# Attention stage of a two-block layer: scores issued three pairs ahead instead of two, four buffers for the unscaled probabilities

## The chip, the cores and the metric

The kernel runs on one core of a Trainium2 chip. The metric is the device time of one execution in microseconds (us), as the median of several runs. Engines are named as the profile names them: PE is the matrix engine (PEld its weight loads), DVE the vector engine, ACT the scalar engine, POOL the GpSimd engine, SP the engine that issues most transfers.

## The reference

The program computes two transformer blocks on 512 tokens of width 1024, in float32. The first block is a feed-forward network, a hybrid mixer, and a second feed-forward network. The second block is a pooling and mLSTM layer. The change lies in the mixer alone, in its softmax attention, which is this part of the reference:

```python
s = jnp.einsum('bqgrd,bkgd->bgrqk', qs, kw).astype(f32)
s = s - slopes[:, :, None, None] * dist_w.astype(f32)
s = jnp.where(mask_w, s, NEG_INF)
p_w = jax.nn.softmax(s, axis=-1)
o_win = jnp.einsum('bgrqk,bkgd->bqgrd', p_w.astype(vw.dtype), vw)
...
o = gb[..., 0:1] * o_cmp + gb[..., 1:2] * o_slc + gb[..., 2:3] * o_win
```

There are 8 query heads in 2 groups of 4, head size 64. With 512 tokens both the selected branch and the window branch are plain causal attention, each over its own keys and values, and each is multiplied by its own gate. A third, compressed branch adds one small product per head. Beside them stands a gated linear attention of 4 heads, worked in chunks of 64 tokens.

## The kernel before, in words

The program is written by hand for each engine: every engine has its own list of instructions, which it works in order, and semaphores join the lists. Nothing is scheduled by a planner, so the order in the loops below is the order on the chip.

Most of the time goes to the dense products. Their weights arrive by SP in units of 512 KB, ACT makes the rounded high half (w_hi, line 1162), POOL the rest (w_lo, line 471), and PE runs three products for each (lines 516 to 518).

The attention stage works on 32 pairs. PAIRS (line 346) runs over the head j of a group (4), the branch b (2) and the block qt of 128 queries (4). A pair is the same work for both groups g. Its width w is (qt + 1) * 128 keys, so the widths 128, 256, 384, 512 recur in turn: pair m has width 128 when m is a multiple of 4, and 512 when m leaves 3. The steps of pair m are:

- scores(m) on PE (line 772): queries by keys into the bank ps[:, g]. There is one bank for each group, so the scores of pair m wait until the maxima of pair m - 1 have been taken (neg_done, line 771).
- negative(m) on DVE (line 1847): reads that bank, adds the distance bias, writes the negated score to a buffer prob and its minimum to nmax. The buffers are a ring of RING pairs, so negative(m) also waits for the turn of pair m - RING (line 1846). At the first pair of each head, biases(j) (line 1835) rewrites the bias first.
- exponent(m) on ACT (line 1348): the exponential in place, its sum to psum_l.
- finish(m) on DVE (lines 1857 and 1861): reciprocal of the sum, then scale by it and by the gate.
- turn(m) on PE (line 786): transposes of 128x128 into the bank ps[:, 2 + g]. It waits for finish(m), and for the copy of pair m - 1 out of the same bank.
- copy(m) on ACT (line 1359): from that bank to one of three buffers for turned probabilities.
- values(m) on PE (line 796), two pairs after the turn. The eighth pair of each head adds the compressed product (line 804). Before the next head's first values, PE waits for the head's result to leave the bank: head_of on ACT (line 1364), then tail_of on DVE (line 1867).

The steps of the linear attention are dealt out among the first 24 pairs by linear(m), six slots for each block of 128 tokens. In it ACT takes squares (line 1370), DVE masks and copies (lines 1874, 1891, 1897), and after pair 23 ACT takes a square root (line 1375), for which it loads another function table and then the exponential's table again. Then POOL scales the result (line 490), and PE turns it (line 856).

The loop of each engine over m (before the change; lines 879, 1382 and 1927) is:

- PE: scores(m + 2), linear(m), values(m - 2), turn(m). In the pairs with m % 8 == 2 (m > 2) the turn comes before the values. At m = 0, after the scores, PE also turns the linear values 2 and 3.
- ACT: exponent(m + 2), at m = 0 the two copies of the turned linear values (line 1309), copy(m), and what falls to this m of head_of, the squares, the root.
- DVE: finish(m), at m = 0 the last projection tile, tail_of where due, negative(m + 2) with biases where a head begins, linear(m).

Scores 0 and 1, and their maxima and exponentials, are taken earlier, beside the last projection tiles.

Of the kernel before, what the change touches and what calls it, by code (L numbers as in the profile page):

```python
# [38 lines left out]
NH, NG, DH = 8, 2, 64  # L39
# [21 lines left out]
    return t if t < MT_Q else t - HPG  # L61


RING = 3
POOL_ADDS = 4
PV_BANK = 4
HALF_BANK, ADD_BANK = 5, 7
# [69 lines left out]
def build(nc, dram, out):  # L137
    with ExitStack() as ctx:
# [14 lines left out]
        scr = sb("scr", [P, DC, T])  # L153
# [42 lines left out]
        w1 = sb("w1", [P, 2, CMP_BLOCK // 2, CMP_HID], F32, own)  # L196
        own.close()
        pc_t = sb("pc_t", [P, NH, T], F32, mixer)
        third_t = pc_t[:, 4:4 + NG, :]
        gel_four, pc_t = pc_t[:, NG, 0:NG * HPG * NC32].rearrange("p (g n) -> p g n", g=NG), pc_t[:, 0:NG, :]  # L200
        own = ExitStack()
        gtmp = sb("gtmp", [P, 8, T], F32, own)
# [11 lines left out]
        c_sum = sb("c_sum", [P, TT * NH], F32, mixer)  # L214
        nmax = sb("nmax", [P, 2 * RING], F32, mixer)
        psum_l = sb("psum_l", [P, 2 * RING], F32, mixer)
# [61 lines left out]
        kst_tok = proj[:, 0:2, :].rearrange("p a t -> p (a t)").rearrange("p (q d) -> p q d", q=TT)  # L278
        k_in, q_in = proj[:, kept(MT_GK):kept(MT_GK) + 2, :], proj[:, kept(MT_GQ):kept(MT_GQ) + 2, :]
        o_tok = proj[:, kept(MT_GV):kept(MT_GV) + GH, :]  # L280
        square_junk = scr[:, 2 * RING, :]
        gated_v = proj[:, kept(MT_GR):kept(MT_GR) + GH, :]

        rows_of = [d_mat[:, 0, :], d_mat[:, 1, :], h_sum[:, 0, :], h_sum[:, 1, :]] + [
# [62 lines left out]
        NPAIR = len(PAIRS)  # L347
        PER_J = NPAIR // HPG
# [155 lines left out]
        def _(pe):  # L504
# [271 lines left out]
            def attention():  # L776
# [100 lines left out]
                        linear_turn(m - 26)  # L877

                for m in range(NPAIR):
                    if m + 2 < NPAIR:  # L880
                        scores(m + 2)
                    if m == 0:
                        pe.wait_ge(pct_done[0], 1)
                        turn_linear_values(2)
                        turn_linear_values(3)
                    linear(m)
                    late = m % PER_J == 2 and m > 2
                    if late:
                        turn(m)
                    if m >= 2:  # L890
                        values(m - 2)
                    if not late:
                        turn(m)
# [261 lines left out]
        def _(act):  # L1155
# [195 lines left out]
            def attention():  # L1351

                def copy(m):
                    w = (PAIRS[m][2] + 1) * P
                    if m >= 3:
                        act.wait_ge(pv_done, m - 2)
                    for g in range(NG):
                        act.wait_ge(turn_ready, 2 * m + g + 1)
                        nc.scalar.activation(turned(m, g)[:, 0:w], ps[:, 2 + g, 0:w], ACT.Copy
                                             ).then_inc(prob_t_done, 1)  # L1360

                def head_of(j):
                    act.wait_ge(oc_done, j + 1)
                    nc.scalar.activation(o_hi[:, j, :], ps[:, PV_BANK, :], ACT.Copy).then_inc(o_hi_done, 1)

                def linear_squares(tt):
                    act.wait_ge(a_used, 2 * tt + 1)
                    for h, m, half in HEADS_OF:
                        k, at = 2 * half + m, O_AT + m * P
                        nc.scalar.activation(square_junk[:, k * P:(k + 1) * P], ps[:, HALF_BANK + half, at:at + P], ACT.Square,  # L1370
                                             accum_out=g_col[:, tt * GH + k:tt * GH + k + 1]).then_inc(gsq_done, 1)

                def linear_root():
                    act.wait_ge(gsq_done, GH * TT)
                    nc.scalar.activation(g_col[:, :], g_col[:, :], ACT.Sqrt, scale=1.0 / GDV, bias=c_("eps")
                                         ).then_inc(grms_done, 1)

                def linear_head(h):
                    act.wait_ge(go_done, TT)
                    nc.scalar.activation(h_hi[:, 4 + h, :], gated_v[:, h, :], ACT.Copy).then_inc(go_hi, 1)  # L1380

                for m in range(NPAIR):
                    if m + 2 < NPAIR:
                        exponent(m + 2)
                    if m == 0:
                        linear_values(2)
                        linear_values(3)
                    copy(m)
                    if m % PER_J == 1 and m > 1:
                        head_of(m // PER_J - 1)  # L1390
                    if m % LIN_SLOTS == 4 and m < TT * LIN_SLOTS:
                        linear_squares(m // LIN_SLOTS)
                    if m == 23:
                        linear_root()
                    if m >= 30:
                        linear_head(m - 30)
                load_root()
                for h in range(2, GH):
                    linear_head(h)
                head_of(HPG - 1)  # L1400
# [253 lines left out]
        def _(dve):  # L1654
# [196 lines left out]
            def attention():  # L1851
# [75 lines left out]
                for m in range(NPAIR):  # L1927
                    finish(m)
                    if m == 0:
                        take(22, 23)  # L1930
                    if m % PER_J == 2 and m > 2:
                        tail_of(m // PER_J - 1)
                    if m + 2 < NPAIR:
                        if (m + 2) % PER_J == 0:
                            biases((m + 2) // PER_J)
                        negative(m + 2)
                    linear(m)
                tail_of(HPG - 1)

# [498 lines left out]
```

## Time and profile before

| | us |
|---|---|
| median of 3 runs | 1676.01 |
| lowest and highest | 1674.09, 1678.9 |
| the profiled execution | 1678.87 |
| its span, first to last instruction | 1677.1 |
| mean granted PE clock of the span | 0.995 of full |
| attention stage, on PE | about 527.8 to 622.4 |

The span is what the trace covers, and 1.77 us lie around it. All start times below count from the start of the span. In a row of the timeline the bracket at the end is the time that the engine stood idle just before the instruction, and what released it. The end of a PE instruction is modelled, and neighbouring ones overlap a little; the chain of work lists them without the overlap.

### The profile page before, as it was taken

The numbers are of one execution on the slowest core, as the hardware profiler recorded it, in microseconds if no ns is written. First come the engines' busy times: TensorE is split into PE (matmuls) and PEld (weight loads), VectorE is DVE, ScalarE is ACT, GpSimd is POOL, SyncE is SP. The second block draws the span as 40 slices with busy tenths as digits, with TensorE's granted clock in tenths as the row PEclk, the third lists the DMA queues.
The fourth block names the chain that finished last, engine by engine and source line by source line (L and its number), as shares of the span: only waits on it lengthen the run. The fifth ranks groups of instructions, "written<-read, shape, count | busy, mean of one in ns | idle before, by whom it ended". The sixth has DMA issues, their size and how long they took to land.

```text
span 1677.1 us, 22221 instructions
## 1 busy us (share of the span) xinstructions
PE 1652.7 (99%) x7820; PEld 1341.6 (80%) x7820; DVE 717.9 (43%) x1149; ACT 645.0 (38%) x998; POOL 648.7 (39%) x278
## 2 busy tenths in 40 slices
PE   7999999999999999999999999999999999999998
PEld 6888888887887668888888888888888888888886
DVE  4333330204535866333332033577678731553222
ACT  5322331323425763332232133574544522444432
POOL 3444444443332024444444444432322324444444
PEclk9999999999999999999999999999999999999999
DMA  4322332225222002232232233222112112332322
GB/s 167 100 99 89 100 100 88 100 88 176 76 80 72 2 1 88 88 100 97 91 100 100 88 100 101 88 88 76 63 63 75 63 63 88 120 106 88 100 92 96
DMA packets 41955, 149.28 MB, mean 89 GB/s; under 512 B 4784, under 2 KB 4912, under 8 KB 41648
## 3 DMA queue, kind: packets, MB, share of 16 engines
q1 hardware_dynamic: 40112, 142.37, 25.3%
q10 hardware_dynamic: 1792, 6.21, 1.1%
q8 instruction: 35, 0.57, 0.1%
q14 instruction: 16, 0.13, 0.0%
HBM read 145.41 MB, written 2.10 MB: 88 GB/s over the span
## 4 chain that ended last, share of the span: by engine, by line
PE 92%; issue 4%; DVE 2%; POOL 1%; ACT 1%; DVEq 0%; POOLq 0%; ACTq 0%
PE ps L516 21%; PE ps L517 20%; PE ps L518 20%; PE ps L622 5%; PE ps L624 5%; PE ps L623 5%; PE ps L1018 1%; PE ps L1030 1%; PE ps L772 1%; PE ps L786 1%; POOL w_lo L471 1%; PE ps L796 1%; PE ps L936 1%; PE ps L938 1%; PE ps L937 1%
## 5 line engine op out<-in xcount | busy, mean ns | idle before, releaser
L471 POOL TENSOR_TENSOR w_lo<-w_raw,w_hi 128x1024 fp32r<-128x1024 f32 x262 | 633.9, 2420 | 933.0 <-ACT w_hi L1162 925.9
L1162 ACT ACTIVATE w_hi<-w_raw 128x1024 fp32r<-128x1024 f32 x260 | 275.7, 1060 | 894.1 <-PE ps L518 650.8
L516 PE MATMUL ps<-h_hi,w_hi 128*128 128x512 f32 x1040 | 408.3, 393 | 2.3 <-POOL w_lo L471 1.8
L517 PE MATMUL ps<-h_lo,w_hi 128*128 128x512 f32 x1040 | 406.1, 390 | 0.0
L518 PE MATMUL ps<-h_hi,w_lo 128*128 128x512 f32 x1040 | 406.0, 390 | 0.0
L516 PEld LDWEIGHTS ps<-h_hi,w_hi 128*128 128x128 f32 x1040 | 195.8, 188 | 46.3 <-issue 2.8
L518 PEld LDWEIGHTS ps<-h_hi,w_lo 128*128 128x128 f32 x1040 | 195.8, 188 | 40.8
L517 PEld LDWEIGHTS ps<-h_lo,w_hi 128*128 128x128 f32 x1040 | 195.8, 188 | 40.0
L516 PE MATMUL ps<-n_hi,w_hi 128*128 128x512 f32 x512 | 207.1, 404 | 0.0
L518 PE MATMUL ps<-n_hi,w_lo 128*128 128x512 f32 x512 | 202.9, 396 | 0.0
L517 PE MATMUL ps<-n_lo,w_hi 128*128 128x512 f32 x512 | 202.8, 396 | 0.0
L624 PE MATMUL ps<-hid_hi,w_lo 128*128 (+1 forms) x352 | 139.2, 395 | 0.0
L622 PE MATMUL ps<-hid_hi,w_hi 128*128 (+1 forms) x352 | 139.1, 395 | 0.0
L623 PE MATMUL ps<-hid_lo,w_hi 128*128 (+1 forms) x352 | 139.1, 395 | 0.0
L518 PEld LDWEIGHTS ps<-n_hi,w_lo 128*128 128x128 f32 x512 | 96.8, 189 | 22.8
L1701 DVE TENSOR_TENSOR silu<-ps,r_row 128x512 f32<-128x512 f32 x44 | 30.4, 692 | 197.2 <-PE ps L518 193.8
L517 PEld LDWEIGHTS ps<-n_lo,w_hi 128*128 128x128 f32 x512 | 96.9, 189 | 22.1
L516 PEld LDWEIGHTS ps<-n_hi,w_hi 128*128 128x128 f32 x512 | 96.7, 189 | 21.9
L1716 DVE SCALAR_TENSOR_TENSOR x<-ps,x 128x512 f32<-128x512 f32 x16 | 11.1, 693 | 200.0 <-PE ps L624 199.8
L1706 DVE TENSOR_TENSOR hid_lo<-hid,hid_hi 128x512 f32 x44 | 70.8, 1610 | 40.2 <-ACT hid_hi L1220 40.2
L622 PEld LDWEIGHTS ps<-hid_hi,w_hi 128*128 128x128 f32 x352 | 66.1, 188 | 16.0
L624 PEld LDWEIGHTS ps<-hid_hi,w_lo 128*128 128x128 f32 x352 | 66.1, 188 | 16.0
(323 smaller groups left out, 1850.0 us busy)
## 6 DMA issues: line engine op xcount, KB each, us to landing
w_raw<-in_units SPq DMA_DIRECT2D x262, 512.0 KB, 3.3
x<-in_x SPq DMA_DIRECT2D x4, 512.0 KB, 7.2
w<-in_w ACTq DMA_DIRECT2D x1, 2048.0 KB, 7.8
out<-scr SPq DMA_DIRECT2D x8, 256.0 KB, 2.0
scr<-proj ACTq DMA_DIRECT2D x8, 128.0 KB, 3.9
inv_count<-in_inv_count ACTq DMA_DIRECT2D x1, 1024.0 KB, 5.1
const<-in_const SPq DMA_DIRECT2D x1, 772.0 KB, 10.2
cbias<-in_cbias ACTq DMA_DIRECT2D x1, 512.0 KB, 9.9
```

The source lines that it names most:

```text
L471: nc.gpsimd.tensor_tensor(w_lo[:, slot, :], w_raw[:, slot, :], w_hi[:, slot, :].bitcast(F32), ALU.subtract).then_inc(w_lo_done, 1)
L516: nc.tensor.matmul(ps[:, bank, :], whi, hi[:, k, :], start=(n == 0), stop=False)
L517: nc.tensor.matmul(ps[:, bank, :], whi, lo[:, k, :], start=False, stop=False)
L518: mm = nc.tensor.matmul(ps[:, bank, :], wlo, hi[:, k, :], start=False, stop=(n == DC - 1))
L622: nc.tensor.matmul(acc, w_hi[:, slot, at:at + P], mv_hi, start=start and kk == 0, stop=False)
L623: nc.tensor.matmul(acc, w_hi[:, slot, at:at + P], mv_lo, start=False, stop=False)
L624: mm = nc.tensor.matmul(acc, w_lo[:, slot, at:at + P], mv_hi, start=False, stop=stop and kk == 1)
L772: nc.tensor.matmul(ps[:, g, 0:w], queries[r, j, qt * P:(qt + 1) * P], tile_((MT_KS, MT_KW)[b])[r, 0:w], start=True, stop=True).then_inc(sc ...
L786: mm = nc.tensor.transpose(ps[:, 2 + g, at], prob[:, 2 * (m % RING) + g, at], ident)
L1162: nc.scalar.activation(w_hi[:, slot, :], w_raw[:, slot, :], ACT.Copy).then_inc(w_hi_done, 1)
L1701: chain.link(nc.vector.tensor_tensor(silu[:, f, :], ps[:, 5 + 2 * f, :], r_row[:, :], ALU.mult))
L1706: nc.vector.tensor_tensor(hid_lo[:, at, :].rearrange("p a t -> p (a t)"), hid[:, f, :], hid_hi[:, at, :].rearrange("p a t -> p (a t)").bit ...
```

## The change

RING goes from 3 to 4, and scores, maxima and exponentials run AHEAD = 3 pairs ahead of the turn. The third pair ahead is opened at m = 0, where each engine now does pair 2 and pair 3 in one go. Values stay two pairs behind the turn, with three buffers for turned probabilities as before. The ring of four pairs takes all 8 tiles of scr, so the junk output of the squares, which lay in the seventh, moves to an unused tile of pc_t. The banks are as before, and nmax and psum_l grow by 2 columns each.

```diff
-RING = 3
+RING = 4
+AHEAD = 3
...
-        third_t = pc_t[:, 4:4 + NG, :]
+        third_t, spent = pc_t[:, 4:4 + NG, :], pc_t[:, 6, :]
...
-        square_junk = scr[:, 2 * RING, :]
+        square_junk = spent
...
                 for m in range(NPAIR):
-                    if m + 2 < NPAIR:
-                        scores(m + 2)
+                    if m == 0:
+                        scores(2)
+                    if m + AHEAD < NPAIR:
+                        scores(m + AHEAD)
                     if m == 0:
                         pe.wait_ge(pct_done[0], 1)
                         turn_linear_values(2)
...
                 for m in range(NPAIR):
-                    if m + 2 < NPAIR:
-                        exponent(m + 2)
+                    if m == 0:
+                        exponent(2)
+                    if m + AHEAD < NPAIR:
+                        exponent(m + AHEAD)
                     if m == 0:
                         linear_values(2)
                         linear_values(3)
...
-                    if m + 2 < NPAIR:
-                        if (m + 2) % PER_J == 0:
-                            biases((m + 2) // PER_J)
-                        negative(m + 2)
+                    if m == 0:
+                        negative(2)
+                    if m + AHEAD < NPAIR:
+                        if (m + AHEAD) % PER_J == 0:
+                            biases((m + AHEAD) // PER_J)
+                        negative(m + AHEAD)
                     linear(m)
```

## Rows read from the trace of the kernel before

**Rows 1.** The page: busy time of each engine, share of the span, instructions
```profile
PE 1652.7 (99%) x7820; PEld 1341.6 (80%) x7820; DVE 717.9 (43%) x1149; ACT 645.0 (38%) x998; POOL 648.7 (39%) x278
```

**Rows 2.** Windows, attention stage: busy of PE, PEld, DVE, ACT, POOL; clock, DMA
```profile
527.80:622.40 94.60, 91.55 (x817) 60.21 (x816) 73.82 (x250) 70.81 (x230) 9.04 (x7) 0.98 0.02 7
```

**Rows 3.** Waits, 527 to 623: who waited for whom, us in total, times, longest
```profile
ACT scr L1348 <- DVE nmax L1847: 18.3, 24, 1.4
...
DVE scr L1847 <- PE ps L772: 8.8, 10, 2.0
```

**Rows 4.** Chain of work, 560 to 569: start, us, what; overlap taken out
```profile
560.70 0.67 PE ps L772 x4
...
562.99 0.85 PE ps L772 x4
...
565.22 0.37 PE ps L786 x2
565.59 1.08 PE ps L772 x4
...
567.12 1.02 PE ps L796 x16
568.14 0.59 PE ps L786 x4
568.73 0.42 PE ps L772 x4
```

**Rows 5.** Timeline, opening of the stage: start, us, engine, line, operation, idle before
```profile
528.82 0.56 DVE L1847 CUSTOM_DVE_ANT_0 scr<-ps,bias 128x384 f32<-128x384 f32 x1
...
529.17 2.36 POOL L471 TENSOR_TENSOR w_lo<-w_raw,w_hi 128x1024 fp32r<-128x1024 f32 x1 [4.30 <-ACT w_hi L1162]
...
529.97 2.04 DVE L1861 TENSOR_SCALAR scr<-scr,psum_l,gate_tok 128x256 f32<-128x256 f32 x2
...
530.63 1.06 ACT L1309 ACTIVATE gv_tok<-ps 128x512 f32<-128x512 f32 x2
...
531.74 0.65 PE L825 MATMUL ps<-gv_tok,proj 64*64 64x128 f32 x8 [0.65 <-ACT gv_tok L1309]
...
534.32 1.16 PE L835 MATMUL ps<-gv_tok,intra 128*128 128x128 f32 x8 [0.27 <-DVE intra L1874]
```

**Rows 6.** Groups by form, 534 to 598: count, busy us, mean ns of one, idle before
```profile
L1847 DVE CUSTOM_DVE_ANT_0 scr<-ps,bias 128x512 f32<-128x512 f32 x10 | 6.5, 689 | 4.7 <-PE ps L772 4.7
...
L1861 DVE TENSOR_SCALAR scr<-scr,psum_l,gate_tok 128x256 f32<-128x256 f32 x10 | 3.7, 410 | 0.2
...
L1348 ACT ACTIVATE scr<-scr,nmax 128x512 f32<-128x512 f32 x11 | 7.9, 724 | 3.6 <-DVE nmax L1847 3.6
```

**Rows 7.** Timeline, the other places where PE waits, before the root and after
```profile
545.84 0.88 DVE L1835 TENSOR_SCALAR bias<-const 128x512 f32<-128x512 f32 x2
...
547.10 0.91 PE L772 MATMUL ps<-proj,queries 64*128 64x256 f32 x4 [0.29 <-DVE nmax L1847]
...
560.26 0.44 PE L796 MATMUL ps<-pc_t,v_tok 128*64 128x128 f32 x4 [0.55 <-DVE o_lo L1867]
...
617.09 0.68 PEld L786 LDWEIGHTS ps<-const,scr 128*128 128x128 f32 x6 [0.35 <-DVE scr L1861]
```

**Rows 8.** Timeline around the square root, 598 to 604
```profile
598.81 1.28 ACT L1375 ACT_TABLE_LOAD   x1
...
598.94 0.30 PE L786 MATMUL ps<-const,scr 128*128 128x128 f32 x1 [0.18 <-ACT pc_t L1359]
...
600.76 2.25 DVE L1861 TENSOR_SCALAR scr<-scr,psum_l,gate_tok 128x256 f32<-128x256 f32 x2
...
602.94 0.42 ACT L1359 ACTIVATE prob_t<-ps 128x128 f32<-128x128 f32 x2
...
603.33 0.63 PE L786 MATMUL ps<-const,scr 128*128 128x128 f32 x4 [0.90 <-ACT prob_t L1359]
```

**Rows 9.** Windows, PE after that wait: length, busy, granted clock, DMA
```profile
604.00:609.00 5.00, 5.00 (x26) 0.66 0.01 2
```

## Prediction, made before the changed kernel was run

> **What bounds the kernel now.** I read the page first. PE is busy for 99% of the span [rows 1], so a change elsewhere counts only where PE waits for it. Then I cut out the attention stage, the only place that the diff touches. It lasts 94.60 us, and PE is busy in 91.55 of them [rows 2]. So PE stands idle for 94.60 - 91.55 = 3.05 us. That is the first number that matters: an edit that only lets work start earlier can win no more than this, 0.18% of the run.
>
> The busy PE might hide more, since its ends are modelled. The Trainium skill ("Perfetto Trace Analysis", Identifying the Most-Contended Engine) warns that busy matmul time is a poor measure of headroom. The chain of work answers that here: its pieces on PE follow each other without a hole, for example 565.22 + 0.37 = 565.59 [rows 4].
>
> Second, the waits of the stage. If distance were short, DVE would wait for exponentials before finish(m). No such wait is in the list. What is there is ACT waiting 18.3 us for maxima, and DVE waiting 8.8 us for scores [rows 3]. Both wait on something that comes from PE, directly or through DVE. The prefetch of two pairs is already long enough, and the helpers idle because PE paces them.
>
> Third, the timeline at each place where PE waits. There are five kinds, and their idle times are the stage's 3.05 us within rounding and overlap: the opening (0.65 and 0.27, [rows 5]), the rewritten bias (0.29), the head's result (0.55 at one head; the others show less), the last pairs (0.35 on the weight loads, some 0.2 net) [rows 7], and the square root (0.90, 0.18 and a smaller one just ahead of it, [rows 8]). After the root PE runs at a mean granted clock of 0.66 for 5 us, at 1.2 GHz for most of them [rows 9]. That costs 5 x 0.34 = 1.7 us.
>
> **The change part by part.** No instruction is added or removed: 32 pairs have the same scores, maxima, exponentials, turns and values as before, and no transfer moves. Only order changes, so every term is a difference of a wait. Scores cost 0.42, 0.67, 0.85 and 1.08 us at widths 128 to 512 [rows 4]. PE does one more pair of scores before any given turn, and gets it back at the end, so shifts by this are no cost.
>
> There is still one bank per group for scores. So scores(m + 3) must wait for negative(m + 2), which DVE issues just where it issued negative(m + 1) before: after finish(m - 1). PE's wait for maxima keeps its place. What grows is the time from exponent to finish, where nobody waits. I cost that part at nothing, in steady state. The moved junk tile and the wider nmax change no instruction's shape: nothing as well. The fourth buffer keeps negative(m + 3) waiting for turn(m - 1), the same turn as before, long done.
>
> Opening (m = 0). Now scores(3) stands ahead of the turns of linear values, negative(3) behind negative(2), and exponent(3) ahead of the two gv_tok copies. Negative(2) begins at 528.82 and takes about 1.05 for both groups, so to 529.9 [rows 5]. Scores(3) follow group by group from 529.4 to 530.5. PE meanwhile has nothing else, as its linear turns are queued behind them. Negative(3) runs 530.1 to 531.4 (2 x 0.689), exponent(3) 530.9 to 532.4 (2 x 0.724 and a read) [rows 6]. The gv_tok copies then take 1.06 [rows 5] and end near 533.5, so that L825 starts near 533.6 instead of 531.74: 1.86 later. Of this PE has used 0.42 for scores(4), which is moved work, not loss. The mask wait of 0.27 (0.35 with overlap) ends in the delay, and some 0.2 of slack between L825 and the next turn go too. Net: 1.86 - 0.42 - 0.35 - 0.2 = +0.9 us. Bounds: 0.2, if the copies come earlier than I think, to 1.6, if nothing is absorbed.
>
> On the DVE, finish(1) used to take 2.04 us here for two instructions, against 2 x 0.41 when alone [rows 5, 6]; it ran beside POOL's w_lo, which lasted to 531.5. Now finish(1) comes after negative(3), at 531.4, when POOL is done. The Trainium skill ("SBUF — State Buffer", Who interferes with whom) says that such a DVE instruction and POOL share a port pair as an exclusive lock. By that rule, the trace agrees. It saves DVE 1.2 us there, but PE waits for ACT in that stretch, so I give it nothing.
>
> Bias. The 0.88 us of biases stood between a 384-wide turn and the next scores, and PE lost 0.29 (0.36 with overlap) at one head [rows 7]. They move one pair up. There the next scores are preceded by 1.02 of 512-wide values and a turn of 0.59 [rows 4], and DVE has time: -0.3 us (0 to -0.36).
>
> Head's result. PE waits at values(8) for bank 4, 0.55 (0.63 with overlap) [rows 7]. Scores(13), 0.67, replace scores(12), 0.42, ahead of it, filling 0.25. The other two heads wait less. DVE's tail_of now delays a wider negative, which can give 0.1 back. Sum: -0.2 us (-0.5 to +0.3).
>
> Square root. ACT works without a pause from the squares of pair 22 through the root to copy(24). The queue gets exponent(26) ahead of copy(23), where 25 was, and exponent(27) ahead of copy(24), where 26 was. Each is one width step more, so +0.25 us each. The first moves with PE's own extra scores; the second delays copy(24), on which turn(25) waits at 603.33 [rows 8]. PE's own work in between shrinks, as scores(27) and scores(28), 1.08 + 0.42, replace scores(26) and scores(27), 0.85 + 1.08 [rows 4]: 0.43 less. So the wait at turn(25) grows from 0.9 to about 1.6, and net of the scores moved ahead the turn comes about +0.35 us late (0 to +0.8). DVE's finish(25), 2.25 us beside POOL [rows 8], stays the next to be late.
>
> End. No scores are left at pair 29. The wait of the last turns for finish goes away, since negative(31) no longer stands before it: -0.2 us (0 to -0.35).
>
> Sum: 0.9 - 0.3 - 0.2 + 0.35 - 0.2 = +0.55, say +0.5. Against the profiled execution's own 1678.87 that is 1679.4. That execution lies 2.86 above the median of 1676.01, and carries nothing here that the others need not have, so against the median it is 1676.5.
>
> **The rivals.**
>
> 1. All the stage's waits go, because slack on ACT and DVE grows at last: -3.05, and with no wait before it the slow clock goes too, -1.7. Together -4.75, or 1671.3. Against it: the opening and the root are waits behind queued ACT work, which the change lengthens. That the granted clock follows the wait is what [rows 8, 9] show.
>
> 2. The clock falls once more. By the times above, PE is idle in the opening for some 0.7 us before scores(3) and for 1.2 us before L825, close together, where it had 0.65 and 0.27; at 603 a wait of 0.9 came before 1.2 GHz. One more such stretch costs 1.7: 1676.5 + 1.7 = 1678.2. The Trainium skill ("TensorE: Matmul & The Clock Gate", What's actually happening) says that a monitor gates the clock by how busy PE has been. By that rule both longer waits speak against this change; it would give the same 1678.2.
>
> 3. Slower, by bunching on ACT. The 512-wide exponent now stands directly before copy(m) for m = 0, 4 ... 28, eight pairs, where before it stood at m = 1, 5 and so on. The next turn needs that copy. From the first group's scores to the end of the copy I get 0.1 + 0.69 for its maxima, 2 x 0.72 + 0.2 for the exponentials [rows 6] and 0.42 for a 128-wide copy [rows 8]: 2.85 us. In that time PE has its own work: the second group's scores 0.54, values 0.81, turn 0.37, scores 0.42, values 1.02 [rows 4] (0.81 is the 384-wide step, between 0.59 and 1.02): 3.16 us. It decides when this slack of 0.3 is gone. Should the handovers take 1.0 more, PE loses about 0.7 in each of eight pairs: +5.6, with the rest 1682.1.
>
> 4. The change doesn't do what it says: three pairs of distance exist on paper, but the single score bank keeps DVE and ACT where they were. That is contained in my forecast, and gives 1676.5 less the small terms: 1676.0.
>
> **How the numbers follow.** My forecast, with rival 4 in it: 0.69. Rival 1, or most of it: 0.12. Rival 2: 0.13. Rival 3: 0.06. The three runs before spread from 1674.09 to 1678.9, so the measured median can move by a microsecond or two without cause. The range reaches from rival 1 to somewhat under rival 3: 1671.5 to 1681.0. A measurement of this kernel can tell 0.3% from no change, that is 5.0 us. Rival 1 gives just under that, so faster has 0.04. Slower is rival 3, or rival 2 more than once: 0.06. Same: 0.90.
>
> **What would show it.** Right: in the changed trace the stage lasts 94 to 96 us. L825 first starts near 533.6, after a PE wait for gv_tok of over 1 us. The first bias no longer has PE waiting behind it. Turn(25) waits 1.3 to 2 us and the clock falls after it as before. DVE's waits for PE's scores and ACT's for maxima stay near 9 and 18 us. Wrong: an opening without a longer wait, regular waits of PE for prob_t at every fourth pair (rival 3), a second stretch at 1.2 GHz (rival 2), or a stage under 92 us (rival 1).

## The result, and the profile after

| | before | after |
|---|---|---|
| median, us | 1676.91 (20 runs) | 1679.22 (20 runs) |
| lowest and highest | 1674.09, 1678.9 | 1676.39, 1682.66 |
| the profiled execution | 1678.87 | 1681.47 |
| its span | 1677.1 | 1679.7 |

The ratio of after to before is 1.0015, with a 95% interval of 1.0009 to 1.0022. The change costs 2.3 us. That is under the 0.3% that the prediction set as its bound, but the interval leaves out 1.

The page of the changed kernel, first its span and then the busy times that answer to [rows 1]:

```profile
span 1679.7 us, 22219 instructions
...
PE 1656.1 (99%) x7820; PEld 1344.0 (80%) x7820; DVE 718.6 (43%) x1149; ACT 645.5 (38%) x998; POOL 649.8 (39%) x278
```

The counts are those of before. PE's busy time grew by 3.4 us with the same 7820 matmuls. Part of it is a lower clock, and part is waits that lie inside a row and count as busy, as the second profile of this kernel will show. The windows of the attention stage answer to [rows 2] and [rows 9]. The columns are the stretch, its length, busy time of PE, PEld, DVE, ACT and POOL, and then the granted clock:

```profile
527.20:624.90 97.70, 93.78 (x817) 62.49 (x816) 73.53 (x250) 71.06 (x230) 9.14 (x7) 0.97 0.02 7
534.00:539.00 5.00, 5.00 (x31) 3.54 (x30) 3.83 (x13) 1.99 (x8) 0.00 (x0) 0.66 0.00 2
606.00:611.00 5.00, 4.00 (x20) 2.89 (x22) 4.63 (x15) 3.90 (x14) 2.47 (x3) 0.66 0.00 2
```

The stage takes 97.7 us instead of 94.6. PE idles in 97.70 - 93.78 = 3.9 of it, where it was 3.05. And there are two stretches at a mean clock of 0.66, most of each at 1.2 GHz, where before had one: the old one behind the root and a new one at 534, behind the opening.

The waits of the stage answer to [rows 3]:

```profile
ACT scr L1351 <- DVE nmax L1852: 17.4, 22, 1.3
...
DVE scr L1852 <- PE ps L773: 10.8, 11, 2.4
```

ACT still waits for maxima and DVE for scores, for nearly as long as before. Nobody waits for an exponential, as nobody did. A third pair of distance had nothing to hide.

The timeline of the opening answers to [rows 5]. The columns are start, length, engine, line, operation, and in brackets the idle time just before and what ended it:

```profile
528.77 1.60 PE L773 MATMUL ps<-proj,queries 64*128 64x512 f32 x4 [0.65 <-DVE nmax L1852]
...
529.93 0.69 DVE L1852 CUSTOM_DVE_ANT_0 scr<-ps,bias 128x512 f32<-128x512 f32 x1 [0.74 <-PE ps L773]
...
531.36 0.73 DVE L1866 TENSOR_SCALAR scr<-scr,psum_l,gate_tok 128x256 f32<-128x256 f32 x2
...
532.09 1.06 ACT L1312 ACTIVATE gv_tok<-ps 128x512 f32<-128x512 f32 x2
...
533.20 0.65 PE L826 MATMUL ps<-gv_tok,proj 64*64 64x128 f32 x8 [1.16 <-ACT gv_tok L1312]
```

Scores(3), maxima(3) and exponent(3) all go ahead of the gv_tok copies. PE runs out of work behind scores(4) and waits 1.16 us, where it had 0.65.

The square root, which answers to [rows 8]:

```profile
604.21 2.25 DVE L1866 TENSOR_SCALAR scr<-scr,psum_l,gate_tok 128x256 f32<-128x256 f32 x2
...
605.18 0.72 ACT L1351 ACTIVATE scr<-scr,nmax 128x512 f32<-128x512 f32 x1
...
606.60 0.42 ACT L1362 ACTIVATE prob_t<-ps 128x128 f32<-128x128 f32 x2
...
607.00 1.09 PE L787 MATMUL ps<-const,scr 128*128 128x128 f32 x4 [1.70 <-ACT prob_t L1362]
```

Exponent(27), 512 wide, now stands ahead of copy(24), and turn(25) waits 1.70 us where it waited 0.90.

**Marks for the comparison.** Each head ends with a compressed product (line 804 before, 805 after), and PE works in one fixed order. So the starts of these four products, counted from the start of scores(2) at 527.87 and 527.21, cut the stage into parts that can be laid side by side. In after they stand at these lines (the timeline of PE, one line from each of four stretches):

```profile
559.42 1.07 PE L805 MATMUL ps<-pc_t,vc_tok 32*64 32x512 f32 x4
...
582.44 1.07 PE L805 MATMUL ps<-pc_t,vc_tok 32*64 32x512 f32 x4
```

The third and the fourth start at 604.23 and 623.98. Before, the starts were 556.79, 579.32, 601.36 and 621.44. This gives the following parts, in us. The columns after the first two are experiments, told below. Their parts come from their own timelines in the same way. A slow stretch behind the root lies in the last part of all but copies first, so that part, and the stage, are not like for like there.

| part, up to | before | after | after, again | copies first | four buffers alone |
|---|---|---|---|---|---|
| first product | 28.92 | 32.21 | 30.67 | 29.48 | 28.92 |
| second | 22.53 | 23.02 | 23.01 | 23.02 | 22.52 |
| third | 22.04 | 21.79 | 21.79 | 21.79 | 22.04 |
| fourth, and to the next stage | 21.08 | 20.75 | 20.84 | 19.74 | 21.06 |
| the stage | 94.57 | 97.77 | 96.31 | 94.03 | 94.54 |

The first part of the changed kernel holds one more scores step of 0.42 us than that of before, and the last part one less.

### The profile page after: what moved, and what is told of

It is laid out like the page before. It is cut to its first block, busy times and chain, and to the rows that moved or that the text cites. A ratio compares the mean times of both kernels' runs of the same rounds, so it can differ in the third digit from the quotient of the medians.

```text
span 1679.7 us, 22219 instructions
## 1 busy us (share of the span) xinstructions
PE 1656.1 (99%) x7820; PEld 1344.0 (80%) x7820; DVE 718.6 (43%) x1149; ACT 645.5 (38%) x998; POOL 649.8 (39%) x278
## 4 chain that ended last, share of the span: by engine, by line
PE 93%; issue 4%; DVE 1%; ACT 1%; POOL 1%; DVEq 0%; POOLq 0%; ACTq 0%
PE ps L517 21%; PE ps L519 20%; PE ps L518 20%; PE ps L624 5%; PE ps L625 5%; PE ps L623 5%; PE ps L773 1%; PE ps L1021 1%; PE ps L1033 1%; PE ps L787 1%; PE ps L797 1%; POOL w_lo L472 1%; PE ps L939 1%; PE ps L940 1%; PE ps L941 1%
## 5 line engine op out<-in xcount | busy, mean ns | idle before, releaser
L624 PEld LDWEIGHTS ps<-hid_lo,w_hi 128*128 128x128 f32 x352 | 66.1, 188 | 16.1
```

The lines of the kernel that those rows point to most:

```text
L624: nc.tensor.matmul(acc, w_hi[:, slot, at:at + P], mv_lo, start=False, stop=False)
```

## The experiments

Theory A, the forecast's: what matters is the opening, where the order puts one pair's scores, maxima and exponentials ahead of the copies. Theory B: the steady state got slower. Theory C: the slow clock behind the opening is the main cost, and it comes from the length of the waits. Every kernel is the changed one with the edit shown, unless it says that it starts from before.

**Opening alone.** Pairs 2 and 3 are opened at m = 0 as in the changed kernel. Then m = 1 opens nothing, and the rest runs two pairs ahead as before.

```diff
-                    if m + AHEAD < NPAIR:
-                        scores(m + AHEAD)
+                        scores(3)
+                    elif 2 <= m and m + 2 < NPAIR:
+                        scores(m + 2)
```

with the same for exponent and negative.

> Pairs 2 and 3 are opened together at m = 0 as in the changed kernel, and from m = 2 on the distance is two pairs as before. My theory: all of the 2.3 us is lost in the opening, about 0.9 to 1.0 as longer waits (before scores(3), before the first L825 product) and 1.7 as a second stretch at 1.2 GHz right behind them. Then this kernel is 2.3 to 2.8 us slower than before, with the slow stretch at about 8 us after scores(2). Rival, the steady distance of three pairs costs it (bunching on ACT, waits for prob_t): then this kernel is within 0.5 us of before.

Measured: 1679.12 us (11 runs) beside 1676.4, ratio 1.0013 (1.0003 to 1.0024). The timeline and one window (with PE alone) of its opening:

```profile
528.51 1.60 PE L773 MATMUL ps<-proj,queries 64*128 64x512 f32 x4 [0.65 <-DVE nmax L1854]
...
532.94 0.65 PE L826 MATMUL ps<-gv_tok,proj 64*64 64x128 f32 x8 [1.58 <-ACT gv_tok L1313]
```

```profile
534.00:539.00 5.00, 5.00 (x34) 0.66 0.01 2
```

The first part is 32.20 us, against 32.21 in after, but it holds no extra scores step: it is 32.20 - 28.92 = 3.28 longer than before, where after is 32.21 - 0.42 - 28.92 = 2.87 longer. The difference is its longer wait, 1.58 for 1.16, as it takes the 0.42 of scores(4) later. So opening one more pair at m = 0 is enough for the whole loss of that part. From there on this kernel runs two pairs ahead, and its second and third parts, 22.52 and 22.05, are those of before. The median is 2.7 us above before, in the 2.3 to 2.8 that I had expected, but its profile owes some of that to chance: the last part, whose order is that of before, took 22.55 instead of 21.08. The window there (PE alone) shows a slow stretch of twice the length:

```profile
606.00:616.00 10.00, 10.00 (x55) 0.66 0.01 2
```

**Copies first.** Three pairs ahead as in the change, but the linear values' turns and copies stand ahead of scores(3) and exponent(3).

```diff
                         scores(2)
-                    if m + AHEAD < NPAIR:
-                        scores(m + AHEAD)
-                    if m == 0:
                         pe.wait_ge(pct_done[0], 1)
                         turn_linear_values(2)
                         turn_linear_values(3)
+                    if m + AHEAD < NPAIR:
+                        scores(m + AHEAD)
```

with exponent(m + AHEAD) on ACT put behind linear_values in the same way.

> Distance three throughout, but at m = 0 PE turns the linear values before scores(3), and ACT copies them before exponent(3). My theory (loss in the opening only): the first L825 product waits no longer than before, the clock stays at 2.4 GHz there, and the time is 0 to 0.6 us below before. Rival (steady distance): still 1.5 to 2.3 us above before.

Measured: 1677.98 us, ratio 1.0002 (0.9993 to 1.0011). The timeline of its opening:

```profile
529.03 1.10 PE L773 MATMUL ps<-proj,queries 64*128 64x128 f32 x4 [0.25 <-DVE nmax L1850]
530.06 0.65 PE L826 MATMUL ps<-gv_tok,proj 64*64 64x128 f32 x8
```

Line 826 starts 530.06 - 525.25 = 4.81 us after scores(2), with no wait before it. In after it was 533.20 - 527.21 = 5.99. The first part falls to 29.48: 1.19 under after's second execution, 2.73 under the first. So the order at m = 0 is the largest single cost. The second and third parts, 23.02 and 21.79, are those of after to the hundredth, so they don't depend on the opening. I had expected 0 to 0.6 us below before, and the runs don't show that: the loss was not in the opening alone.

**Four buffers alone**, from before: RING = 4 and the moved junk tile, with a distance of two pairs.

```diff
-RING = 3
+RING = 4
...
-        square_junk = scr[:, 2 * RING, :]
+        square_junk = spent
```

> Only the ring of four buffers and the moved junk tile, with the distance of two pairs as before. All my theories: no difference, within 0.5 us of before. Rival, the place of the buffers or the shifted tiles matter: up to 2.3 us above before.

Measured: 1675.82 us, ratio 0.9992 (0.9982 to 1.0002), and all its parts are those of before within 0.02. The buffers cost nothing and give nothing, as expected. The difference lies in the distance.

**Filled wait.** Nine transposes of a constant into a bank that is free there, just ahead of the wait for gv_tok. Nobody reads what they give.

```diff
                             if tt == 0:
+                                pe.wait_ge(gv_copied, 2)
+                                for k in range(9):
+                                    nc.tensor.transpose(ps[:, ADD_BANK, k % 4 * P:(k % 4 + 1) * P], c_("ident"), ident)
                                 pe.wait_ge(gv_copied, GH)
```

> The changed kernel with nine 128-column transposes of a constant on PE, about 1 us, into a free bank in the place where PE waits for gv_tok; their result is not used. The wait itself keeps its length. My theory, that a second stretch at 1.2 GHz after that wait is 1.7 us of the 2.3: the clock stays up at 535 to 539, and the time is about 0.6 us above before. Rival, the clock is a bystander and the waits alone cost it: 2.3 us above before, with or without the slow stretch.

Measured: 1678.04 us, ratio 1.0004 (0.9995 to 1.0013). The timeline and a window (PE alone):

```profile
531.58 1.20 PE L869 MATMUL ps<-const 128*128 128x128 f32 x9
532.81 0.65 PE L826 MATMUL ps<-gv_tok,proj 64*64 64x128 f32 x8
```

```profile
533.00:538.00 5.00, 5.00 (x46) 1.00 0.07 28
```

Line 826 starts 6.00 after scores(2), as in after (5.99). But the clock stays full, and the first part is 30.66 instead of 32.21. That would make the clock's share 1.55 us. The stage takes 96.30 us, 1.73 more than before, where I had expected 0.6. Whether the filler is what kept the clock up, one execution cannot say. So the next runs asked how steady the changed kernel is itself.

**The changed kernel again**, with nothing edited.

> The changed kernel once more. So far its profile shows 1.2 GHz at 535 to 539, and the profile of another kernel with the same opening shows the same waits and no fall. Theory A: the fall behind the opening waits comes in some executions only, and the change costs 1.6 to 1.7 us in every execution, and 1.5 more where the clock falls: a median 1.7 to 2.5 us above before, and a first product of the compressed branch either 30.7 or 32.2 us after scores(2). Theory B, the fall belongs to the code: 32.2 again.

Measured: 1678.55 us (12 runs) beside 1676.39, ratio 1.001 (0.9999 to 1.0021). Its windows (PE alone), the stage and the five microseconds where the first profile had 0.66:

```profile
528.41:624.70 96.29, 92.37 (x817) 0.98 0.02 7
535.20:540.20 5.00, 5.00 (x44) 1.00 0.01 2
```

and its timeline at the gv_tok wait:

```profile
529.98 1.60 PE L773 MATMUL ps<-proj,queries 64*128 64x512 f32 x4 [0.65 <-DVE nmax L1852]
...
534.40 0.65 PE L826 MATMUL ps<-gv_tok,proj 64*64 64x128 f32 x8 [1.16 <-ACT gv_tok L1312]
```

The waits are the same two, 0.65 and 1.16, and the clock doesn't fall. So in the same kernel the fall comes in some executions and not in others. And PE is busy for 92.37 us of the stage, 0.82 more than before, with one slow stretch in each: most of that must be waits inside rows. What every execution pays is 96.31 - 94.57 = 1.74 us, both profiles having the fall behind the root. A fall in the opening adds 32.21 - 30.67 = 1.54.

**Both waits filled**: filled wait, and five such transposes between scores(2) and scores(3).

```diff
                         scores(2)
+                        pe.wait_ge(gv_copied, 2)
+                        for k in range(5):
+                            nc.tensor.transpose(ps[:, ADD_BANK, k % 4 * P:(k % 4 + 1) * P], c_("ident"), ident)
```

> The changed kernel with constant transposes on PE in both waits of the opening (five before scores(3), nine before the first L825 product), so that PE is hardly idle there; their result is not used. Both theories: no fall in the opening, first compressed product 30.7 us after scores(2) as the waits themselves stay. Under theory A the timed runs lie about 0.7 us under those of the changed kernel, under theory B 1.5.

Measured: 1678.0 us, ratio 1.0008 (0.9999 to 1.0016). Its marks are those of filled wait within 0.02, with no fall in the opening. The two filled kernels and after again lie within 0.6 us, and their intervals overlap. Whether the filler keeps falls away isn't shown. Three profiles have the changed kernel's own waits: after had a fall, after again and copy(24) first (below) had none. The two with filler had none either. The two kernels with a wait longer than that, opening alone with 1.58 and longer wait (next) with 2.20, both had one.

**Longer wait.** On ACT, two more copies of 512 columns into unused tiles ahead of the gv_tok copies, which PE then gets a microsecond later.

```diff
                     if m == 0:
+                        for idle in (pc_3, pc_7):
+                            nc.scalar.activation(idle, c_("dist"), ACT.Copy)
                         linear_values(2)
```

> The changed kernel with two copies of a constant on ACT ahead of the gv_tok copies, about 1.2 us more for PE to wait at the first L825 product; their result is not used. If idle time of PE in the opening is what brings the clock down, the fall comes here more often than in the changed kernel: first compressed product 33.2 to 33.5 us after scores(2), timed runs 1.2 to 2 us above the changed kernel. If the wait does not pass on one to one, less than 1.0.

Measured: 1680.35 us, ratio 1.0023 (1.0013 to 1.0034). The timeline and a window (PE alone):

```profile
530.60 1.11 PE L826 MATMUL ps<-gv_tok,proj 64*64 64x128 f32 x8 [2.20 <-ACT gv_tok L1312]
```

```profile
531.00:541.00 10.00, 10.00 (x72) 0.69 0.00 1
```

The wait grew by 1.04 us, but the first part by 34.69 - 30.67 = 4.02. The rest is the clock: 10 x (1 - 0.69) = 3.1 us. I had expected a part of 33.2 to 33.5, so the slow stretch was twice as long as I thought. That length is from one profile, and its last part has such a stretch too, 22.28 us for the 20.84 of after again, behind a wait of 1.70 that the edit doesn't touch. The timed runs do not hang on one profile: the median is 1.8 us above after again for a wait 1.04 longer, and the mean granted clock listed with the runs is 0.9947 over 11 runs, against 0.9954 over the 32 of the changed kernel. By these runs a longer wait on PE costs more than its own length, in clock.

**Copy(24) first.** ACT takes copy(24) ahead of exponent(27).

```diff
+                    if m == 24:
+                        copy(m)
                     if m + AHEAD < NPAIR:
                         exponent(m + AHEAD)
...
-                    copy(m)
+                    if m != 24:
+                        copy(m)
```

> The changed kernel, but at pair 24 ACT copies the turned probabilities before exponent(27) and the table load that it needs, so that turn(25) no longer waits behind them. If the longer queue on ACT is what keeps turn(25) late (its wait grew from 0.90 to 1.70 us), the wait now ends with DVE's finish(25), which runs beside POOL and finishes near 606.4 on the changed kernel's clock instead of 607.0: the stage gets 0.5 to 1.1 us shorter, and the rest of the wait stays. If ACT's queue is not what holds it: no difference in the stage.

Measured: 1676.84 us beside 1677.27, ratio 1.0005 (0.9993 to 1.0016). The timeline behind the root:

```profile
600.21 0.44 PE L787 MATMUL ps<-const,scr 128*128 128x128 f32 x2 [0.16 <-DVE scr L1869]
601.26 0.44 PE L787 MATMUL ps<-const,scr 128*128 128x128 f32 x2 [0.61 <-DVE scr L1869]
```

and the wait and the clock in the opening, which is the changed kernel's:

```profile
529.52 0.66 PE L826 MATMUL ps<-gv_tok,proj 64*64 64x128 f32 x8 [1.17 <-ACT gv_tok L1312]
```

```profile
529.50:534.50 5.00, 4.98 (x44) 1.00 0.13 51
```

The wait of 1.70 for prob_t is gone, so the queue on ACT was its cause. In its place stand 0.16 and 0.61 for DVE's finish(25), which runs beside POOL. That is the step I had named as next to be late. The stage is 95.66 us, 0.65 less than after again. The clock fell behind the root here too.

**The same edit on before.**

> The same edit on the kernel before, ahead of exponent(26). Its wait of 0.90 at turn(25) ends with finish(25) too, so the stage gets about 0.5 us shorter, and within the runs no difference can be told (under 0.1%).

Measured: 1677.12 us, ratio 1.0005 (0.9994 to 1.0016). The stage is 94.14 us. The profile has no fall in it, and before had one, so the comparison flatters the edit. No gain can be told.

**The best of three, and of two.** Copies first and copy(24) first together, and on DVE the reciprocal of g_col moved behind finish(25), so that POOL starts later. The second kernel is before with the two root edits.

```diff
-                    elif m == 24:
-                        dve.wait_ge(grms_done, 1)
-                        nc.vector.reciprocal(g_col[:, :], g_col[:, :]).then_inc(grstd_done, 1)
...
                     finish(m)
+                    if m == 25:
+                        dve.wait_ge(grms_done, 1)
+                        nc.vector.reciprocal(g_col[:, :], g_col[:, :]).then_inc(grstd_done, 1)
```

> Distance three, with the linear values copied before pair 3 is opened, copy(24) before exponent(27), and DVE's reciprocal for the linear part after finish(25) instead of before it, so that POOL starts behind finish(25). My theory, that the waits at the opening and at the root and the two stretches at 1.2 GHz behind them are all that there is to gain: no wait over 0.4 us left on PE, no granted clock under 1.00 in the stage, stage 92 to 93.5 us against 94.6 before and 97.8 changed, time 1 to 3 us below before. If the steady distance of three costs more than I take it for, it stays at 94 or above.

> The same two edits at the root (copy(24) first, reciprocal after finish(25)) on the kernel before, distance two, three buffers. If the third pair of distance is worth nothing, this gets the same or more than the version with distance three: stage 91.5 to 93 us, time 1.5 to 3 us below before. If the third pair carries exponents over the root's table loads, PE waits here for finish(26), 0.5 to 1.5 us, and the version with three is ahead.

Measured: 1677.16 us, ratio 1.0002 (0.9993 to 1.0011), and 1676.92 us, ratio 1.0001 (0.999 to 1.0012). The timeline of the first, and then of the second:

```profile
603.50 0.84 PE L787 MATMUL ps<-const,scr 128*128 128x128 f32 x6 [1.08 <-ACT prob_t L1361]
```

```profile
602.70 0.85 PE L786 MATMUL ps<-const,scr 128*128 128x128 f32 x6 [1.15 <-DVE scr L1864]
```

Turn(25) no longer waits, and turn(26) does instead, for over a microsecond. Behind the root the edits only hand the wait on by one pair. I had expected stages of 92 to 93.5 and 91.5 to 93 us. They took 95.33 and 93.70, the first with a slow stretch behind the root and the second with none. Neither kernel can be told from before.

**Short scores late.** Copies first, and in the pairs m = 5, 9, 13 ... the 128-wide scores(m + 3) come behind values(m - 2) instead of ahead of them, so that PE has the 512-wide values to do while DVE takes the 512-wide maxima.

```diff
+                    short = m % TT == 1 and m > TT
+                    if m + AHEAD < NPAIR and not short:
+                        scores(m + AHEAD)
                     linear(m)
...
                         values(m - 2)
+                    if m + AHEAD < NPAIR and short:
+                        scores(m + AHEAD)
```

> Distance three with the linear values copied first, and from pair 5 on the 128-wide scores of every fourth pair are issued behind values(m - 2) instead of ahead of it, so that the 512-wide maxima have values and not only a 128-wide turn to run beside. If this cover is what the steady distance lacks, PE's waits inside the 128-wide scores (0.28 at pairs 5 and 17, 0.16 at pair 25) go, and the stretch between the first and second compressed products falls from 23.0 to 22.5 to 22.8 us. If the later scores make their own maxima late, it stays at 23.0 or grows, above all at pairs 9, 17 and 25, where the values take 2 us.

Measured: 1678.19 us, ratio 1.001 (1.0 to 1.0019). Its marks are 29.06, 52.64, 75.21 and 95.63. The first part is 0.42 under copies first, but that is again scores(12), now behind the mark. The second and the third are 23.58 and 22.57, where copies first has 23.02 and 21.79. The wait inside the short scores went, which takes 0.42 for scores(20) again instead of 0.71, so it was the order that made it. Others came in its place: scores(13) took 1.19 instead of 0.63, and turn(18) 1.24 instead of 0.81. This exchange gets nothing back.

## Why the prediction came out as it did

The time lies in the range and the sign is the one that I gave the largest chance. The size was not: I forecast +0.55 us, and the medians differ by 2.3. That the time lies in the range is in part the range's width, 9.5 us: it would have held a loss several times my sum. And the absolute numbers moved under it, as the median of before is 1676.91 over 20 runs where I started from 1676.01 over three.

Of the three theories, A explains most of what every execution pays and B the rest: of 1.74 us, 1.36 is lost in the opening and 0.38 behind it, as worked out below. C, the clock, comes on top in some executions. By the steps of the forecast:

**What bounds the kernel.** Right. PE is the bound, the helpers wait for it as before, and none of the changed kernel's waits is for an exponential.

**Opening, +0.9 (0.2 to 1.6).** The mechanism was right and the size too small. Line 826 starts 5.99 us after scores(2). I forecast 533.6 - 527.87 = 5.73, and the wait over 1 us is there, as 1.16. Scores(3) start when I said, 528.77 - 527.21 = 1.56 after scores(2), but DVE begins maxima(3) 529.93 - 528.77 = 1.16 behind that, where I had 0.7. The loss is best read where scores(4) and its wait are past on both sides, at the start of line 835. That is 534.32 - 527.87 = 6.45 after scores(2) before [rows 5], and in after again, where the clock doesn't fall, 536.85 - 528.41 = 8.44:

```profile
536.22 0.70 PE L773 MATMUL ps<-proj,queries 64*128 64x256 f32 x4
536.85 1.16 PE L836 MATMUL ps<-gv_tok,intra 128*128 128x128 f32 x8
```

Scores(5), moved ahead of it, are 0.63 of that, so the opening costs 8.44 - 6.45 - 0.63 = 1.36. The mask wait went as forecast. The 0.2 of slack behind line 825 that I counted on did not: turn(1) follows it after 1.23 us in both kernels. Copies first takes 30.67 - 29.48 = 1.19 of the 1.36 away. Finish(1) took 0.73 us instead of 2.04, as forecast. The Trainium skill ("SBUF — State Buffer", Who interferes with whom) calls the port pair of DVE and POOL an exclusive lock, and this row agrees. It gave PE nothing, also as forecast.

**Bias, -0.3.** Right. The wait behind the bias went: turn(6) and the wait behind it took 547.10 - 545.93 = 1.17 us before, and turn(6) takes 0.80 in after. The timeline of after, where the bias is rewritten now:

```profile
544.72 0.69 DVE L1852 CUSTOM_DVE_ANT_0 scr<-ps,bias 128x512 f32<-128x512 f32 x1
...
545.18 0.78 PE L773 MATMUL ps<-proj,queries 64*128 64x128 f32 x4
...
545.88 1.09 PE L797 MATMUL ps<-prob_t,v_tok 128*64 128x128 f32 x16
...
546.18 0.88 DVE L1840 TENSOR_SCALAR bias<-const 128x512 f32<-128x512 f32 x2
```

PE is not idle behind 546.18. But look at scores(8) at 545.18: 128 columns, next PE line 0.70 us later, where the chain of before had 0.42 for them [rows 4]. Their second group waits for the 512-wide maxima of pair 7, which begin at 544.72 and end at 545.41. This wait has no bracket, as it lies inside a row of four matmuls. These 0.28 take back what the bias gave: behind the opening the first part changed by 30.67 - 0.42 - 28.92 - 1.36 = -0.03 in all.

**"I cost that part at nothing, in steady state".** This is the step that failed. I argued that PE's wait for maxima keeps its place. It keeps its place before scores(m + 3), but what PE does in that time changed. Ahead of the 128-wide scores, DVE has two 512-wide maxima to take, 2 x 0.69 = 1.38 and a handover. Before, PE had 512-wide values and a turn of 256 beside them, 1.02 + 0.59 = 1.61 [rows 4]. Now it has 384-wide values and a turn of 128, 0.81 + 0.37 = 1.18. I had the terms of both sums and used them for ACT alone, in rival 3. Four buffers alone has the order of before, and its scores(20) take what the chain of before gave:

```profile
579.68 0.66 PE L786 MATMUL ps<-const,scr 128*128 128x128 f32 x4
580.26 0.49 PE L772 MATMUL ps<-proj,queries 64*128 64x128 f32 x4
580.68 0.65 PE L825 MATMUL ps<-gv_tok,proj 64*64 64x128 f32 x8
```

The step from 580.26 to 580.68 is 0.42. In after, the same scores(20) show the stretched form, 581.41 - 580.71 = 0.70:

```profile
580.34 0.44 PE L787 MATMUL ps<-const,scr 128*128 128x128 f32 x2
580.71 0.78 PE L773 MATMUL ps<-proj,queries 64*128 64x128 f32 x4
581.41 1.09 PE L797 MATMUL ps<-prob_t,v_tok 128*64 128x128 f32 x16
```

It comes at scores(8), (20) and, with 0.16, (28). Ahead of scores(12), (16) and (24) PE also has a step of the linear attention to do, and there the scores take 0.42, 0.33 and 0.42 in after again, without a wait.

**Head's result, -0.2.** The wait itself shrank as I said, from 0.55 to 0.37:

```profile
562.89 0.44 PE L797 MATMUL ps<-pc_t,v_tok 128*64 128x128 f32 x4 [0.37 <-DVE o_lo L1872]
563.26 1.23 PE L773 MATMUL ps<-proj,queries 64*128 64x384 f32 x4
564.42 0.66 PE L797 MATMUL ps<-prob_t,v_tok 128*64 128x128 f32 x8
```

The next row gives it back. Scores(14) take 564.42 - 563.26 = 1.16 where a 384-wide step is 0.85 [rows 4]: they wait for negative(13), which DVE begins only at 562.75, behind tail_of. I had named this with 0.1; it is 0.31. Scores(17), behind the second rewritten bias, took 0.82 where they had 0.63. Together with the stretched scores(20) the second part grew by 23.01 - 22.53 = +0.48. The third shrank, 21.79 - 22.04 = -0.25, but not at a head's result. The gain lies just ahead of the root, where the waits around 598.94 [rows 8] went: before, values(22) and turn(24) took 599.17 - 597.51 = 1.66 us, and in after again 1.30, the whole of it and a little more.

**Square root +0.35 and end -0.2.** Right together. The last part of after again is 20.84, before's is 21.08, and with the moved scores the difference is 20.84 + 0.42 - 21.08 = +0.18, against +0.15. The wait is 1.70, where I said about 1.6. Taken alone each is less sure: both profiles have a slow stretch in this part, and the end gave about 0.1, the step ahead of turn(30) falling from 0.57 to 0.48.

The sum of what every execution pays: 1.33 in the first part (1.36 - 0.03), 0.48 - 0.25, and 0.18, which is 1.74, against my 0.55. Of the 1.19 that I was short, 0.70 lies between the opening and the root, where I had -0.3 and -0.2 and nothing for the rest, and the parts give -0.03 + 0.48 - 0.25 = +0.20. 0.46 is the size of the opening.

**Rival 2, one more fall of the clock, 0.13.** True in part of the executions. Its price of 1.7 was about right, as it measured 1.54. It came behind the two longer waits, in the profile of after. My mistake was to take it as something that either is there or isn't: it is a matter of how often. The Trainium skill ("TensorE: Matmul & The Clock Gate", What's actually happening) says that a monitor gates the clock by how busy PE has been. Longer wait agrees in direction, with 2.20 us idle and 0.69 over 10 us. But after and after again have the same two waits and 0.66 against 1.00, so busy time as the rows show it doesn't decide.

The medians differ by 2.3 us. 1.74 is in every execution, and some 0.6 is left for falls that now come more often. That rest is taken by subtraction from medians that move by half a microsecond. The granted clocks listed with the timed runs agree in direction: their mean is 0.9961 over the 102 runs of before that the three rounds of experiments list, and 0.9954 over the 32 runs of the changed kernel. Among the runs of before 0.001 of clock goes with about 1.4 us (figures below), so 0.0007 is an estimated 0.9 us. Where the runs of both list the same clock, from 0.994 to 0.997, the means of the changed kernel are 0.7 to 2.1 us above.

**Rival 1** fell, as the waits of the opening and the root grew. **Rival 3** in its form, PE waiting for prob_t at every fourth pair, did not come; its neighbour, PE waiting for maxima ahead of 128-wide scores, did, at some of these pairs (0.28 at scores(8) and at scores(20), 0.16 at scores(28)) and not 0.7 at all eight. **Rival 4**, three pairs on paper, is right as to DVE and ACT: their waits are 10.8 and 17.4, near the 8.8 and 18.3 of before. I expected a stage of 94 to 96 us. It was 97.77 and 96.31.

## What to carry to other kernels

Before lengthening a prefetch, look for a wait on what is prefetched. If there is none, the longer distance can only rearrange which work stands beside which wait, and each step of a different width has to be laid against its new neighbour, also on the engines that the change isn't about. At the start of such a pipeline, put what the bounding engine needs next ahead of what is prefetched. For differences of 0.1%, mark fixed points in the order of the bounding engine and compare the parts between them, from more than one execution.

## What the runs showed of the hardware

The clock of PE falls to 1.2 GHz for a few microseconds in some executions of a kernel and not in others. The changed kernel's opening had 0.66 over 5 us in one profile and 1.00 in another, with waits of 0.65 and 1.16 in both.

It also falls where the profile shows no wait of PE at all. Some 65 us ahead of the stage, in code that the change doesn't touch, there is a row of 64 matmuls of 32 columns. First that row in the first profile of the changed kernel, then two windows of the same profile, and last the window in copies first (windows with PE alone):

```profile
460.71 5.70 PE L737 MATMUL ps<-kc_t,queries 64*128 64x32 f32 x64
```

```profile
455.00:463.00 8.00, 8.00 (x63) 1.00 0.19 66
462.00:472.00 10.00, 10.00 (x67) 0.66 0.17 52
```

```profile
462.00:472.00 10.00, 10.00 (x90) 1.00 0.17 54
```

PE is shown busy throughout, and the clock is at 0.66 over 10 us in one execution and full in the other. The profile of before has 0.66 there over 5 us. So a wait is not needed for a fall, and what decides whether one comes stays open.

The timed runs follow their granted clock. The 102 runs of before take 1672.7 us in the mean where they list 0.999, 1674.2 at 0.998, 1675.2 at 0.997, 1676.6 at 0.996, 1678.6 at 0.995 and 1679.5 at 0.994. That is most of the spread of this kernel, 1672.6 to 1681.4. So a single profile of a 1.7 ms kernel can mislead by more than this whole change is worth.

A fall costs less where waits follow it. Behind the root the last part has 20.84 us with a fall (after again) and 19.74 without one (copies first), 1.1 and not 1.5 to 1.7. The order there is the same; that the slower PE meets later waits already ended is my explanation, and no run tests it.
